# The last projection of a hybrid encoder: tile pairs as two by two block products with seven products

## The reference

```python
def _odd_mixer(h, w_in, b_in, dw_w, dw_b, ln_g, ln_b, w_out):
    z = h @ w_in + b_in
    a, b, g = _split(z, (CONV_WIDTH, CONV_WIDTH, CONV_WIDTH))
    u = a * jax.nn.sigmoid(b)
    u = lax.conv_general_dilated(...) + dw_b
    u = jax.nn.silu(_layernorm(u, ln_g, ln_b))
    return (u * jax.nn.silu(g)) @ w_out
...
    x = x + gate[:, None, :] * _rmsnorm(y, post_g[layer])
```

## Time and profile before

| | us |
|---|---|
| median of 3 runs | 2308.5 (2306.32 to 2308.62) |
| profiled execution, own time | 2312.47 |
| profiled execution, span | 2310.6 |
| mean granted TensorE clock | 0.989 |
| TensorE busy in the span | 2242.0 (97%) |
| VectorE, ScalarE, GpSimd busy | 1370.0, 1125.9, 900.6 |
| last stage, first output matmul to the end | 2099.9 to 2310.6 |

### The profile page before, as it was taken

The page is one execution under the profiler, slowest core; times in us unless marked ns, Lnnn a source line. Parts: engine busy times, 40 slices in busy tenths (PEclk is TensorE's granted clock), DMA queues, the critical chain, the costliest instruction groups (busy, mean ns, idle before and its releaser), DMA issues. The chain is left out here.

```text
span 2310.6 us, 31013 instructions
## 1 busy us (share of the span) xinstructions
PE 2242.0 (97%) x11298; PEld 1884.8 (82%) x11298; DVE 1370.0 (59%) x2083; ACT 1125.9 (49%) x2095; POOL 900.6 (39%) x665
## 2 busy tenths in 40 slices
PE   5999999999999999999999989998999999999998
PEld 5888888898897788888888878887888888888886
DVE  7333336343435776767677642115999999994442
ACT  5555534222224555555555535556555566663432
POOL 6322222232222111101101023232999999992454
PEclk9999999999999999999999999999999999999999
DMA  7533323534444222222131323331111211145553
GB/s 304 183 136 136 136 78 132 173 120 151 137 149 141 56 65 69 65 69 65 32 83 33 105 105 112 134 118 37 46 55 42 69 55 42 64 167 163 157 172 101
DMA packets 151298, 245.75 MB, mean 106 GB/s; under 512 B 8964, under 2 KB 95236, under 8 KB 146566
## 3 DMA queue, kind: packets, MB, share of 16 engines
q1 hardware_dynamic: 146566, 235.73, 31.0%
q10 hardware_dynamic: 4608, 8.39, 1.0%
HBM read 157.84 MB, written 86.25 MB: 106 GB/s over the span
## 5 line engine op out<-in xcount | busy, mean ns | idle before, releaser
L2410 POOL TENSOR_TENSOR conv_g<-conv_g,product 128x1024 f32<-128x1024 f32 x160 | 385.0, 2408 | 34.2 <-ACT product L2459 24.5
L2554 DVE SCALAR_TENSOR_TENSOR ps_b<-u,cols,ps_b 128x1024 f32<-128x1024 f32 x304 | 391.7, 1288 | 9.2
L2670 PE MATMUL ps_a<-ho_hi,wp_lo 128*128 128x512 f32 x768 | 300.2, 391 | 6.8 <-DVE h_left L2610 6.8
L2671 PE MATMUL ps_a<-h_left,wp_hi 128*128 128x512 f32 x768 | 299.6, 390 | 0.0
L2672 PE MATMUL ps_a<-ho_hi,wp_hi 128*128 128x512 f32 x768 | 299.5, 390 | 0.0
L2459 ACT ACTIVATE product<-u,cols 128x1024 f32<-128x1024 f32 x160 | 183.3, 1151 | 170.3 <-POOL conv_g L2410 169.0
L1771 DVE TENSOR_TENSOR pt_lo<-ps_pt,pt_hi 128x512 fp32r<-128x512 f32 x256 | 176.1, 688 | 136.0 <-ACT pt_hi L1666 134.0
L1666 ACT ACTIVATE pt_hi<-ps_pt 128x512 fp32r<-128x512 f32 x256 | 154.4, 604 | 202.9 <-PE ps_pt L1858 202.1
L1761 DVE TENSOR_REDUCE mx<-ps_s 128x1 f32<-128x512 f32 x248 | 168.2, 683 | 34.3 <-PE ps_s L1850 32.6
L1659 ACT ACTIVATE probs<-ps_s,bias 128x512 f32<-128x512 f32 x248 | 168.8, 700 | 17.6 <-DVE bias L1767 9.3
L2670 PEld LDWEIGHTS ps_a<-ho_hi,wp_lo 128*128 128x128 f32 x768 | 144.6, 188 | 38.6 <-DVE h_left L2610 8.7
(11 more groups left out here) (445 smaller groups left out, 5435.4 us busy)
## 6 DMA issues: line engine op xcount, KB each, us to landing
scratch_ret_pack<-pack SPq DMA_DIRECT2D x14, 1280.0 KB, 5.5
pack<-scratch_ret_pack SPq DMA_DIRECT2D x14, 1280.0 KB, 6.4
ada<-in_ada_w_dram SPq DMA_DIRECT2D x16, 768.0 KB, 6.1
wp_raw<-in_od_w_in_dram SPq DMA_DIRECT2D x24, 512.0 KB, 3.9
xt<-in_x_dram SPq DMA_DIRECT2D x16, 512.0 KB, 6.2
ada<-in_ada_w_dram SPq DMA_DIRECT2D x8, 1024.0 KB, 9.3
mix_e<-scratch_mix SPq DMA_DIRECT2D x16, 512.0 KB, 4.5
x_e<-in_x_dram SPq DMA_DIRECT2D x16, 512.0 KB, 5.0
```

What stands on the lines that cost most here:

```text
L2410: pool.tensor_tensor(half(conv_g, h), half(conv_g, h), product[adds(c, i, h) % 2][:], ALU.add).then_inc(added, 1)
L2554: dve.scalar_tensor_tensor(acc[h], units(c, k, h), params(c, k), acc[h], ALU.mult, ALU.add).then_inc(tap, 1)
L2670: pe.matmul(dst, lo[:, k, :], h_hi[:, k, t], start=k == 0, stop=False)
L2671: pe.matmul(dst, hi[:, k, :], h_lo[:, k, t], start=False, stop=False)
```

## The change

Tiles 0 to 3 keep their 48 matmuls. Tiles 2q and 2q+1, q from 2 to 7, become one product of blocks. The two tiles are the two block rows (A11, A12 and A21, A22, each 128 tokens by 512 channels), the weight's quarters the other matrix. Operand sums: S1 = A21 + A22, S2 = S1 - A11, S3 = A11 - A21, S4 = A12 - S2. Weight sums T1 to T4 likewise, made once from a second copy of the weight, which SP loads in four quarters of 1 MB at the start of the stage. Seven products M1 to M7 of 4 blocks x 3 matmuls (84 for a pair, where two tiles had 96) go into four banks of PSUM, and seven combinations U2, U4, U3, C22, C11, C12, C21 of 512 columns on VectorE add them into res. M1 is first copied out of PSUM by ScalarE. Each of the seven operands is copied to its high part by ScalarE and its residue is made by VectorE, 512 columns at a time. The scaling and the residual addition then work in place on res. The square reads res. The loops are written out, and every engine has a new order. The new diff lines cut to their core (`weight_hi` and `weight_lo` split a weight sum, 2048 columns, as `operand_hi` and `operand_lo` an operand; `store(t)` also issues load_x(t+2); `with_sum` and `with_weight` call `part` with a weight sum or a quarter of the weight):

```diff
+    o.m_lo_raw = o.m_lo
+    o.m_t2 = st.gate[0][:].rearrange("p (k t) -> p k t", t=P)
+    o.m1 = at("m1_o", soon.u1 + 8 * D, (P, BANK))
...
+        PLAIN = 4
...
+        X, Y, PB, Z = [ps_a[:, i * BANK:(i + 1) * BANK] for i in range(4)]
+        M1, M6, M5, M7, M2, M3, M4 = range(7)
+        A11, A12, S2, S1, S3, S4, A22 = range(7)
+        U2, U4, U3, C22, C11, C12, C21 = range(7)
+        T3, T1, T2, T4 = range(4)
...
+        def place(t):
+            return o.m_t if t <= PLAIN or t % 2 == 0 else o.m_t2
...
-            over_tiles(sp, tile)
+            load_g(2)
+            for j in (1, 0):
+                for i in (1, 0):
+                    sp.dma_start(quarter(t_raw, i, j), w_src[i * HK * P:(i + 1) * HK * P, j * HN:(j + 1) * HN]
+                                 .rearrange("(k p) n -> p k n", p=P)).then_inc(t_in[j], 16)
+            load_v(4)
+            load_g(3)
+            store(0)
+            load_v(5)
+            load_g(4)
+            store(1)
+            load_v(6)
+            load_v(7)
+            load_g(5)
+            store(2)
+            load_v(8)
+            load_g(6)
+            load_g(7)
+            store(3)
+            for q in pairs:
+                load_v(2 * q + 5)
+                load_g(2 * q + 4)
+                load_v(2 * q + 6)
+                load_g(2 * q + 5)
+                store(2 * q)
+                store(2 * q + 1)
...
+            for t in range(2):
+                activate(t + 1, t)
+                split(t + 1)
+                square(t, ps_y[t % 2], y_done, t + 1)
+            activate(3, 2)
+            split(3)
+            weight_hi(T3)
+            weight_hi(T1)
+            activate(4, 2)
+            act.wait_ge(m_done, 5)
+            square(2, ps_y[0], y_done, 3)
+            operand_hi(FIRST, A11)
+            operand_hi(FIRST, A12)
+            activate(5, 3)
+            weight_hi(T2)
+            for a in (S2, S1, S3, S4):
+                operand_hi(FIRST, a)
+            weight_hi(T4)
+            square(3, ps_y[1], y_done, 4)
+            operand_hi(FIRST, A22)
+            for q in pairs:
+                n = q + 1
+                act.wait_ge(part_done, parts(q, M1))
+                if q > FIRST:
...
+                act.activation(o.m1[:], X, ACT.Copy).then_inc(m1_kept, 1)
+                if n <= LAST:
+                    activate(2 * n, 2 * q)
+                if n <= LAST:
+                    operand_hi(n, A11)
+                    activate(2 * n + 1, 2 * q)
+                if n <= LAST:
+                    operand_hi(n, A12)
+                    act.wait_ge(m_done, 2 * n + 2)
+                square(2 * q, res[0][:], c_step, combined(q, C12))
+                if n <= LAST:
+                    for a in (S2, S1, S3, S4, A22):
+                        operand_hi(n, a)
+                square(2 * q + 1, res[1][:], c_step, combined(q, C21))
...
+            def multiply(t):
...
+                pool.tensor_tensor(place(t)[:], act_t[:], gt[t % 2][:], ALU.mult).then_inc(m_done, 1)
...
+            for q in pairs:
+                n = q + 1
+                if n <= LAST:
+                    multiply(2 * n)
+                    deviation(2 * n + 1)
+                    multiply(2 * n + 1)
+                    if n < LAST:
+                        deviation(2 * n + 2)
+                rstd(2 * q)
+                add(2 * q)
+                rstd(2 * q + 1)
+                add(2 * q + 1)
...
+            def scaled(t):
...
+                else:
+                    y = res[t % 2][:]
+                    dve.scalar_tensor_tensor(y, y, ry[:], st.gate[1][:], ALU.mult, ALU.mult).then_inc(yn_done, 1)
+            def weight_sum(i):
...
+                if i == T3:
+                    ins = dve.tensor_tensor(t[T3], t[T3], t[T1], ALU.subtract)
...
+                    dve.wait_ge(t_in[0], 32)
...
+                    ins = dve.tensor_tensor(t[T1], t[T1], t[T2], ALU.subtract)
...
+                    dve.wait_ge(t_sum, 2)
+                    ins = dve.tensor_tensor(t[T2], t[T2], t[T3], ALU.add)
...
+                    dve.wait_ge(t_sum, 3)
+                    ins = dve.tensor_tensor(t[T4], t[T4], t[T2], ALU.subtract)
...
+            def operand_lo(q, a):
...
+                dve.tensor_tensor(op_lo[a], src, op_hi[a].bitcast(F32), ALU.subtract).then_inc(alo_done, 1)
...
+            def operand_sums(q):
+                one, two = place(2 * q), place(2 * q + 1)
...
+                dve.wait_ge(m_done, 2 * q + 2)
...
+                dve.tensor_tensor(op_raw[S1], two[:, first, :], two[:, last, :], ALU.add).then_inc(s_sum, 1)
...
+                dve.tensor_tensor(op_raw[S2], op_raw[S1], one[:, first, :], ALU.subtract).then_inc(s_sum, 1)
...
+                dve.tensor_tensor(op_raw[S3], one[:, first, :], two[:, first, :], ALU.subtract).then_inc(s_sum, 1)
...
+                dve.tensor_tensor(op_raw[S4], one[:, last, :], op_raw[S2], ALU.subtract).then_inc(s_sum, 1)
...
+            def combine(q, c):
...
+                u2 = yn[:, 0:HN]
+                left = [one[:, 0:HN] for one in res]
+                right = [one[:, HN:D] for one in res]
+                if c == U2:
+                    dve.wait_ge(part_done, parts(q, M6))
+                    dve.wait_ge(m1_kept, q - FIRST + 1)
...
+                    ins = dve.tensor_tensor(u2, o.m1[:], Y, ALU.add)
+                elif c == U4:
...
+                    dve.wait_ge(c_step, combined(q, U2))
...
+                    ins = dve.tensor_tensor(right[0], u2, PB, ALU.add)
+                elif c == U3:
...
+                    dve.wait_ge(res_stored[1], 16 * q)
+                    ins = dve.tensor_tensor(left[1], u2, Z, ALU.add)
+                elif c == C22:
...
+                    ins = dve.tensor_tensor(right[1], left[1], PB, ALU.add)
+                elif c == C11:
...
+                    ins = dve.tensor_tensor(left[0], o.m1[:], X, ALU.add)
+                elif c == C12:
...
+                    ins = dve.tensor_tensor(right[0], right[0], Y, ALU.add)
+                else:
...
+                    ins = dve.tensor_tensor(left[1], left[1], Z, ALU.add)
...
+            for t in range(2):
+                moments(t + 2)
+                normed(t + 2)
+                split(t + 1)
+                if t == 1:
+                    weight_sum(T3)
+                    weight_sum(T1)
+                scaled(t)
+            moments(4)
+            normed(4)
+            weight_sum(T2)
+            split(3)
+            weight_sum(T4)
+            moments(5)
+            normed(5)
+            weight_lo(T3)
+            scaled(2)
+            operand_lo(FIRST, A11)
+            operand_lo(FIRST, A12)
+            weight_lo(T1)
+            moments(6)
+            operand_sums(FIRST)
+            normed(6)
+            weight_lo(T2)
+            for a in (S2, S1, S3, S4):
+                operand_lo(FIRST, a)
+            scaled(3)
+            operand_lo(FIRST, A22)
+            for q in pairs:
+                n = q + 1
+                if q == FIRST:
+                    weight_lo(T4)
+                combine(q, U2)
+                if n <= LAST:
+                    moments(2 * n + 1)
+                    operand_lo(n, A11)
+                    normed(2 * n + 1)
+                combine(q, U4)
+                combine(q, U3)
+                combine(q, C22)
+                combine(q, C11)
+                if n <= LAST:
+                    operand_lo(n, A12)
+                combine(q, C12)
+                if n <= LAST:
+                    if n < LAST:
+                        moments(2 * n + 2)
+                    operand_sums(n)
+                    if n < LAST:
+                        normed(2 * n + 2)
+                    operand_lo(n, S2)
+                    operand_lo(n, S1)
+                combine(q, C21)
+                scaled(2 * q)
+                if n <= LAST:
+                    for a in (S3, S4, A22):
+                        operand_lo(n, a)
+                scaled(2 * q + 1)
...
+            def part(q, m, a, dst, b_hi, b_lo):
+                pe.wait_ge(alo_done, 7 * (q - FIRST) + a + 1)
+                for k in range(HK):
+                    hi, lo = op_hi[a][:, k, :], op_lo[a][:, k, :]
+                    pe.matmul(dst, lo, b_hi[:, k, :], start=k == 0, stop=False)
+                    pe.matmul(dst, hi, b_lo[:, k, :], start=False, stop=False)
+                    mm = pe.matmul(dst, hi, b_hi[:, k, :], start=False, stop=k == HK - 1)
+                mm.then_inc(part_done, 1)
...
+            for k in range(KD):
+                product(2, 0, k)
+            turn_n(4)
+            turn_v(5)
+            for k in range(KD):
+                mm = product(2, 1, k)
+            mm.then_inc(y_done, 1)
+            turn_n(5)
+            pe.wait_ge(mlo_done, 4)
+            pe.wait_ge(yn_done, 2)
+            for k in range(KD):
+                mm = product(3, 1, k)
+                if k == HK - 1:
+                    mm.then_inc(b12_read, 1)
+            turn_v(6)
```

(129 more changed lines are left out.)

249 lines of the change are left out of this document (147 added, 102 removed).

## The result

The changed kernel takes 2348.9 us (median of 4 runs, 2348.0 to 2351.5) against 2308.6 for the kernel before (4 runs beside them, 2306.3 to 2310.4): ratio 1.0175, interval [1.0163, 1.0187], 40 us slower. The forecast was 2342.5 in a range of 2318 to 2354.

A forecast was written before the change was run, and what follows sets the result against it. TensorE's issue rate was taken to bound the last stage; matmuls -16.4, prologue +15, ring stalls +25.2, end +3.2 and clock +7 sum to +34 on 2308.5, giving 2342.5 us, range 2318 to 2354.

The forecast's parts named there:

- Matmuls, -16.4: Six pairs on TensorE: 84 instead of 96 matmuls each, 72 fewer at 0.228 us, -16.4 us.
- Prologue, +15: Tiles 1 to 4 and the first pair: TensorE waits for VectorE and GpSimd, together 15 us, 10.3 without contention.
- Four ring stalls, 4 x 6.3: TensorE stalls of 6.3 us at turn_n(9), (11), (13), (15), +25.2 us; 22.4 without contention.
- The ring: Closed chain of a pair over TensorE, VectorE and GpSimd between odd turn_n: 28.2 us, 28.9 with contention.
- The clock, 1.75 a long stall, +7: TensorE's clock drops behind the four long stalls, taken as 1.75 us each from 0 to 3.1, +7.
- The end, 13.2 for 10.0: Stretch from the last matmul to the end grows from 10.0 to 13.2 us, +3.2.
- the clock holds: Rival: stalls cost no TensorE clock, the ring alone gives +19.5 to +27; 2320 to 2336 us, chance 0.31.
- Each stall costs 3: Rival: each long stall and the prologue's lose 3 us of clock, 28 for 7; above 2354, chance 0.08.
- TensorE stays the bound: Rival: the pairs' ring is under 22.6 us, +1.8, no change at 2310 us; chance 0.06.
- Faster: Rival: pairs TensorE-bound and the first pair's stalls gone too, -13.2, 2295 us; chance 0.05.
- the signs that the forecast named: Among them: steady pairs' turn_n 28 to 31 us apart, nt waits 5 to 7, last matmul near 2324 to 2332.

The follow-up runs named there:

- e14: e11 with the even tile's turn_v right behind the odd turn_n, its moments behind U4, and S2 and S1 residues ahead of scaled(2q) again; 2320.0 us.
- e1: Changed kernel with dummy identity transposes on TensorE in the stalls ahead of turn_n(4), (6), (7), (9), (11), (13), (15); 2342.2 us.
- e9: Changed kernel without the second weight load and the weight sums T1 to T4; four products take plain quarters, altering the computation; 2339.8 us.
- e2: Changed kernel with only GpSimd's add(2q+1) issued later, behind multiply(2q+4) and deviation(2q+5); 2346.9 us.
- e3: Changed kernel with only TensorE's turn_n(2n+1) issued behind M3 instead of ahead of M2; 2349.4 us.
- e11: Changed kernel with the pair's order rearranged (scaled(2q) straight behind the operand sums) and add(2q+1) behind the next pair's multiply(2q+2) and deviation(2q+3); 2332.8 us.

## Why the prediction was right, and where its sizes were off

Each term as predicted, and measured from the start of the stage in the profile after:

- *Matmuls, -16.4.* 72 fewer, and 22.6 a pair if nothing waits: e14's 23.70 with a stall of 0.87 leaves 22.8.
- *Prologue, +15.* turn_n(7) was forecast at 80.5 and came at 82.5, so 16.9. The stalls themselves are fewer than forecast (3.2, 1.1, 3.8, 0.9 and 1.7 for 2.4, 3.3, 3.8, 1.9 and 3.5, 10.7 for 15). Counted on TensorE the rest is half clock, 5.5; but e1 took 3.9 of that away and turn_n(7) still came at 82.6. So the other engines' chain sets it, and in that chain T4's residue and multiply(6) exclude each other for longer than the forecast had put in (the last section). That 15 comes so near is in part luck. e9 says that 9.1 of the time is the weight sums' doing; their loads aren't late (10.0 from issue to landing in the median, as forecast).
- *Four ring stalls, 4 x 6.3.* They are 6.5, at the transposes that were named. The ring was forecast as 28.9 and is 29.8 (e1): 4 x (29.8 - 22.6) = 28.8 instead of 25.2. **This is the term that was mis-sized.** Its steps were right (in e1, 16.0 from turn_n(9) to add(6) for 15.85 forecast); the contention in it wasn't. I read the earlier trace rows as VectorE working at a quarter of its pace beside GpSimd and so charged scaled(2q+1) with 0.65. In the runs the pace isn't shared: add(2q) stands for the whole row of residues, 1.6, in each of the four ring pairs, and 28.2 + 1.6 = 29.8. The earlier trace rows could not have told this: there GpSimd gets in between two residues, and the one that starts at 1570.21 stands for it and takes 2.87. That is add(12)'s case, where scaled(13) starts 4.36 behind the add's start, not far from the 4.05 that the forecast comes to (2.45 + 0.95 + 0.65); in the ring it is 4.93.
- *The clock, 1.75 a long stall, +7.* 6.7 by e1, nearly all of it behind the four long stalls that the forecast named. But 1.75 was a choice between 0 and 3.1, and that it fits is luck. The profile shows 13.7 lost, but half of it falls where TensorE would have waited.
- *The end, 13.2 for 10.0.* 13.4.

-16.4 + 16.9 + 28.8 + 6.7 + 3.4 = +39.4; the stage grew by 39.85. The rival "the clock holds" is excluded by the windows above: it went to half behind each long stall. "Each stall costs 3" was wrong in its place: the prologue's stalls of 3.2 and 3.8 did bring the clock down, where I had called that weak, but e1 got nothing back there. "TensorE stays the bound" asked for a closing GpSimd part that is not serial; GpSimd's rows from 2226.96 to 2237.91 have add, rstd, add and multiply one behind the other, and it takes e14's order to bring the pairs near TensorE's own 22.6. "Faster" needed stalls under 13.2 in all; there are 36.9. Of the signs that the forecast named, two were off a little: two of the four pairs are over 31 (31.20 and 32.44, of which 1.4 and 2.7 is half clock), and the last matmul is at 2334.0, not 2324 to 2332.

What I underrated is that a ring is not one: with a step taken out, the next ring was only 0 to 1 us shorter (e2, e3, e11), and a moved step could meet the other engine where it had been free (e2).

## What to carry to other kernels

A saving on the engine that sets the pace is worth nothing per loop until the longest closed ring of hand-overs over the other engines is shorter than that engine's own work; add the ring up step by step, and then the second and third ring, before the matmuls that fall away. Where VectorE and GpSimd both take two SBUF tensors, add their times as if they were one engine, and look who starts first. Work made "beside" earlier tiles has a price as soon as it stands ahead of something in an engine's queue: here 9 us for four sums with their splits.

## What the runs showed of the hardware

- VectorE and GpSimd, both with two SBUF inputs, exclude each other in full, whatever the size of what waits: an add of 8 columns took 1.79 us behind three residues; one of 1,024 took 3.98; a scaling that started 0.07 behind a multiply took 3.41 instead of 1.28. Of two single instructions the one that starts first goes first (2214.46 and 2215.59, 2264.12 and 2264.19). Against a row of VectorE instructions both orders happen: GpSimd stood for all three residues in the ring, and got in behind the one that was running at add(12) and in the earlier trace rows; why, no run shows. C11, with one input in PSUM, kept its 0.69 at 2214.92, inside a multiply, in the profile after. A longer chain of it, GpSimd (add(3), multiply(6)) and VectorE (T4's residue) in the profile after:

```profile
2169.87 2.74 POOL L2987 TENSOR_TENSOR res<-yn_o,x_o 128x1024 f32<-128x1024 f32 x1 [1.40 <-DVE yn_o L3042]
2172.57 4.44 POOL L2974 TENSOR_TENSOR m_t<-act_t,gt 128x1024 f32<-128x1024 f32 x1
```

```profile
2170.31 4.45 DVE L3068 TENSOR_TENSOR t_last_lo<-t_last,t_last_hi 128x2048 fp32r<-128x2048 f32 x1
```

The residue (2.28 alone) stands until the add ends at 2172.6 and runs to 2174.8; the multiply (2.34 alone) stands until then and ends at 2177.0.

- TensorE's clock went to 0.50 behind shorter stalls than the earlier trace rows show: behind 3.2 in the profile after and behind 1.98 at 2258.6 in e14, where 2.02 at 2233.8 left it at 1.00, so the stall's length alone doesn't decide:

```profile
2259.00:2262.50 3.50, 3.50 (x18) 3.31 (x17) 2.86 (x5) 2.35 (x7) 0.47 (x1) 0.51 0.62 187
2233.80:2237.30 3.50, 3.50 (x24) 3.19 (x25) 3.50 (x5) 2.39 (x7) 0.86 (x1) 1.00 0.52 152
```

Each time some 3.5 us at half clock followed, 1.7 lost, or twice that. Dummy transposes in the stalls kept it whole, and were worth 6.7 us where TensorE was in the longest ring (e1) and nothing at the transposes ahead of it.
